# One decoder layer on one core: the gate stage in five rounds instead of four, with half of the output normed and stored in the last round

## The chip, the cores and the metric

The kernel runs on one core of a Trainium2 chip. The metric is the device time of one execution in microseconds (us). Five engines work side by side, each on its own list of instructions in order: PE (matrix products into the PSUM banks, with a separate track PEld for its weight loads), DVE (VectorE), ACT (ScalarE), POOL (GpSimd) and SP, which here only issues DMAs. They wait for each other by semaphores alone.

## The reference, cut to what matters

The last two steps of one decoder layer are the stage at issue; D = 2048, 512 tokens, depth 1.

```
h = h + y @ w_out                                     # mixer, before
h = h + square(relu(rmsnorm(h, g_mlp) @ w_up)) @ w_down   # MLP, before
gate = sigmoid(rmsnorm(h, g_ple) @ w_pg)              # w_pg: 2048 x 2048
h = h + gate * (p @ w_pp)                             # p: 512 x 256, w_pp: 256 x 2048
return rmsnorm(h, g_final)                            # mean of squares over 2048 columns
```

Everything is fp32. A product is made of three matmuls (`tri`): each operand is split into a part rounded to fp32r ("hi") and the rest ("lo"), and hi*hi, hi*lo and lo*hi are summed in a bank.

## The kernel before, in words

Tokens lie in four tiles of 128 (t = 0 to 3). In the gate stage h lies with tokens on the partitions, and is updated in 16 blocks: `block_of_h(q, t)` is 128 tokens by the 512 columns of quarter q.

The stage is a loop over the quarters q = 0 to 3. One quarter is nine half units (`GATE_HUS`, pos 0 to 8): eight for `w_pg` (each 256 of the 2048 rows by 512 columns) and, at pos 4, one for `w_pp`. A half unit has one weight half, which ACT copies to `w_hi` (`gate_hi`), DVE subtracts to `w_lo` (`gate_lo`), and PE multiplies with all four token tiles (`gate_half`): 4 tiles x 2 x 3 = 24 matmuls of 128x512, so 6 per tile. There are four slots of `w_hi` and `w_lo`, and `gate_hi` of a half unit waits until PE is done with the one four before:

```
act.wait_ge(half_done, s - 3)      # gate_hi
pe.wait_ge(half_lo, s + 1)         # gate_half
```

After pos 8 of quarter q its banks hold the gate's argument. It is worked off tile by tile while PE multiplies for quarter q + 1: `gate_clamp` (DVE, reads the bank), `gate_exp` (ACT), `gate_inverse` (ACT: a Ln and an Exp), `gate_add` (DVE: two steps of refinement, the product with pp, the sum into h), `square_out` (ACT: squares of the new block, summed into `x_sum`) and `gain_out` (DVE: the block times `g_final`). `gates_of(q, at)` says after which position of the next quarter each engine does which of these; it does them in three portions, at = 2, 3 and 4. The order of DVE and ACT is that of the program text, and nothing in it is skipped: an instruction that waits holds all those behind it.

The last quarter has no next one. Its gates stand behind the loop, then come the row means (`row_mean`), 1/sqrt (`rms_ln_exp` on ACT, `refine` on DVE), the scaling of each token tile of h by its row's factor (DVE t = 0, 1, 2; ACT t = 3), and the four stores of 1 MB each by SP.

```
for t in (0, 3, 1, 2):             # SP, behind the last load
    ... wait for the scaling of tile t
    sp.dma_start(out_tok[:, t, :]..., h[:, :, t * P:(t + 1) * P])
```

`w_pg` comes in 16 loads of 1 MB (a quad: two half units) into a ring of three (`load_quad`); a load is issued when `gate_lo` has read the second half of the quad three before.

## Time and profile before

| | us |
|---|---|
| median of 3 runs (lowest, highest) | 2589.91 (2589.11, 2590.95) |
| the profiled execution | 2590.34 |
| its span, first to last instruction | 2588.6 |
| PE busy in the span | 2506.7 (97%) |
| DVE busy | 1658.9 (64%) |
| ACT busy | 993.0 (38%) |
| POOL busy | 239.2 (9%) |

PE's granted clock is 0.987 of full speed on average. The page's first part gives busy time by engine; its second shows PE at 9 tenths or more in every slice but the first and the last; the last slice has 3 tenths. A time such as 2545.25 below is counted from the start of the span. In a row of the timeline the first number is the start, the second the length, "x3" says that three such instructions are merged, and what stands in brackets is how long the engine was idle before and what released it. In a row of "windows" come PE, PEld, DVE, ACT and POOL busy (with the number of instructions), then PE's granted clock (1.00 is 2.4 GHz, 0.50 is 1.2 GHz), the DMA engines' share and GB/s.

### The profile page before, as it was taken

The numbers are of one execution on the slowest core, as the hardware profiler recorded it, in microseconds if no ns is written. First come the engines' busy times: TensorE is split into PE (matmuls) and PEld (weight loads), VectorE is DVE, ScalarE is ACT, GpSimd is POOL, SyncE is SP. The second block draws the span as 40 slices with busy tenths as digits, with TensorE's granted clock in tenths as the row PEclk, the third lists the DMA queues.
The fourth block names the chain that finished last, engine by engine and source line by source line (L and its number), as shares of the span: only waits on it lengthen the run. The fifth ranks groups of instructions, "written<-read, shape, count | busy, mean of one in ns | idle before, by whom it ended". The sixth has DMA issues, their size and how long they took to land.

```text
span 2588.6 us, 29850 instructions
## 1 busy us (share of the span) xinstructions
PE 2506.7 (97%) x11424; PEld 2067.7 (80%) x11424; DVE 1658.9 (64%) x1995; ACT 993.0 (38%) x1338; POOL 239.2 (9%) x186
## 2 busy tenths in 40 slices
PE   6999999999999999999999999999999999999993
PEld 5788888888777788888888888888888888888883
DVE  5676666687778524444444444469898899894563
ACT  5444444334444213333333333334333333344442
POOL 5111111122023333000000000000000000000000
PEclk8999999999999999999999999999999999999997
DMA  6323223222232432655555555567555655633222
GB/s 213 82 65 81 74 72 81 74 73 76 70 81 74 138 97 81 203 183 176 176 182 182 183 183 182 180 226 258 197 174 195 244 216 207 225 133 111 85 74 65
DMA packets 414844, 366.93 MB, mean 142 GB/s; under 512 B 5356, under 2 KB 352136, under 8 KB 414616
## 3 DMA queue, kind: packets, MB, share of 16 engines
q1 hardware_dynamic: 414648, 365.54, 44.5%
q8 instruction: 67, 1.10, 0.2%
q14 instruction: 33, 0.27, 0.0%
q10 hardware_dynamic: 96, 0.02, 0.0%
HBM read 298.43 MB, written 67.11 MB: 141 GB/s over the span
## 4 chain that ended last, share of the span: by engine, by line
PE 64%; DVE 2%; ACT 1%; issue 0%; POOL 0%; DVEq 0%; POOLq 0%
PE bank L1757 21%; PE bank L1758 21%; PE bank L1759 21%; DVE u_lo L1501 0%; PE bank L1997 0%; PE bank L1953 0%; ACT w_hi L734 0%; DVE w_lo L1141 0%; DVE w_lo L1553 0%; ACT u_hi L901 0%; DVE gate_e L1679 0%; DVE gate_e L1675 0%; DVE gate_e L1673 0%; DVE h L1750 0%; DVE w_raw L1578 0%
## 5 line engine op out<-in xcount | busy, mean ns | idle before, releaser
L1757 PE MATMUL bank<-u_hi,w_hi 128*128 128x512 f32 x2192 | 874.5, 399 | 17.2 <-DVE w_lo L1141 6.3
L1759 PE MATMUL bank<-u_hi,w_lo 128*128 128x512 f32 x2192 | 858.4, 392 | 0.0
L1758 PE MATMUL bank<-u_lo,w_hi 128*128 128x512 f32 x2192 | 857.9, 391 | 0.0
L1757 PEld LDWEIGHTS bank<-u_hi,w_hi 128*128 128x128 f32 x2192 | 414.1, 189 | 112.2 <-issue 13.3
L1758 PEld LDWEIGHTS bank<-u_lo,w_hi 128*128 128x128 f32 x2192 | 414.4, 189 | 87.6 <-issue 4.6
L1759 PEld LDWEIGHTS bank<-u_hi,w_lo 128*128 128x128 f32 x2192 | 413.8, 189 | 87.4
L1141 DVE TENSOR_TENSOR w_lo<-w_raw,w_hi 128x2048 fp32r<-128x2048 f32 x132 | 307.5, 2329 | 209.2 <-ACT w_hi L734 209.1
L1757 PE MATMUL bank<-w_hi,forms 128*128 128x512 f32 x896 | 349.7, 390 | 0.4 <-DVE h L1596 0.4
L1759 PE MATMUL bank<-w_hi,forms 128*128 128x512 f32 x896 | 349.1, 390 | 0.0
L1758 PE MATMUL bank<-w_lo,forms 128*128 128x512 f32 x896 | 349.0, 389 | 0.0
L734 ACT ACTIVATE w_hi<-w_raw 128x2048 fp32r<-128x2048 f32 x137 | 260.5, 1904 | 226.2 <-PE bank L1759 212.2
L989 ACT ACTIVATE w_hi<-ring 128x1024 fp32r<-128x1024 f32 x128 | 136.4, 1066 | 213.6 <-PE bank L1759 146.1
L1757 PEld LDWEIGHTS bank<-w_hi,forms 128*128 128x128 f32 x896 | 168.3, 188 | 35.4 <-issue 0.8
L1759 PEld LDWEIGHTS bank<-w_hi,forms 128*128 128x128 f32 x896 | 168.3, 188 | 34.9
L1758 PEld LDWEIGHTS bank<-w_lo,forms 128*128 128x128 f32 x896 | 168.3, 188 | 34.6
L1516 DVE SCALAR_TENSOR_TENSOR relu<-bank,rs_u 128x512 f32<-128x512 f32 x64 | 44.3, 692 | 225.0 <-PE bank L1759 225.0
L962 ACT ACTIVATE araw<-relu 128x512 f32<-128x512 f32 x64 | 40.5, 633 | 351.2 <-DVE relu L1516 351.2
L1553 DVE TENSOR_TENSOR w_lo<-ring,w_hi 128x1024 fp32r<-128x1024 f32 x128 | 155.7, 1222 | 10.5 <-ACT w_hi L989 10.5
L989 ACT ACTIVATE w_hi<-w_raw 128x1024 fp32r<-128x1024 f32 x96 | 101.8, 1063 | 151.1 <-PE bank L1759 147.8
L689 POOL TENSOR_TENSOR tmp<-b 128x512 f32<-128x512 f32 x84 | 96.6, 1155 | 544.2 <-DVE ql L1251 244.1
L1596 DVE TENSOR_TENSOR h<-h,bank 128x512 f32<-128x512 f32 x224 | 143.3, 682 | 0.0
L1553 DVE TENSOR_TENSOR w_lo<-w_raw,w_hi 128x1024 fp32r<-128x1024 f32 x96 | 117.4, 1223 | 39.1 <-ACT w_hi L989 39.0
(234 smaller groups left out, 2508.8 us busy)
## 6 DMA issues: line engine op xcount, KB each, us to landing
w_raw<-in_w_up SPq DMA_DIRECT2D x64, 1024.0 KB, 6.4
w_raw<-in_w_in SPq DMA_DIRECT2D x57, 1024.0 KB, 5.6
forms_scratch<-stage SPq DMA_DIRECT2D x32, 1792.0 KB, 7.3
forms<-forms_scratch SPq DMA_DIRECT2D x56, 1024.0 KB, 7.2
ring<-in_w_down SPq DMA_DIRECT2D x40, 1024.0 KB, 5.9
w_raw<-in_w_down SPq DMA_DIRECT2D x24, 1024.0 KB, 5.5
w_raw<-in_w_out SPq DMA_DIRECT2D x16, 1024.0 KB, 5.9
ring<-in_w_pg SPq DMA_DIRECT2D x16, 1024.0 KB, 5.0
```

The lines of the kernel that those rows point to most:

```text
L689: pool.tensor_tensor(tmp[:, lv % 2, :].rearrange("q (n c) -> q n c", c=2 << lv), bv, ref, ALU.subtract).then_inc(diff_ready, 1)
L734: act.activation(w_hi[:, unit.slot, :], w_raw[:, unit.slot, :], ACT.Copy).then_inc(w_hi_ready, 1)
L962: act.activation(araw[:, i % 4, :], relu[:, i % 2, :], ACT.Square).then_inc(a_ready, 1)
L989: act.activation(hi_half(s), part(half_of(G, l), i), ACT.Copy).then_inc(half_hi, 1)
L1141: v.tensor_tensor(w_lo[:, unit.slot, :], w_raw[:, unit.slot, :], w_hi[:, unit.slot, :].bitcast(F32), ALU.subtract).then_inc(w_lo_ready, 1)
L1516: v.scalar_tensor_tensor(out=relu[:, i % 2, :], in0=bank[unit.slot][:, :], scalar=0.0, in1=rs_u[:], op0=ALU.max, op1=ALU.mult).then_inc(z_ ...
L1553: v.tensor_tensor(lo_half(s), part(half_of(G, l), l % 2), hi_half(s).bitcast(F32), ALU.subtract)\
L1596: v.tensor_tensor(dst, dst, by_tile(bank[bk + t][:, :]), op).then_inc(added, 1)
L1757: pe.matmul(ps, whi, xhi, start=start, stop=False, skip_group_check=shared)
L1758: pe.matmul(ps, whi, xlo, start=False, stop=False, skip_group_check=shared)
L1759: return pe.matmul(ps, wlo, xhi, start=False, stop=stop, skip_group_check=shared)
```

## The change

The quarter q = 3 is made in two rounds, first for token tiles 0 and 1, then for tiles 2 and 3. Both rounds go through all nine half units, so that each of these weight halves is loaded, copied and subtracted twice (pp's raw half is kept and only split again); a round of two tiles has 12 matmuls in a half unit. The gates of tiles 0 and 1 are worked off in the last round, which also norms, scales (tile 0 on DVE, tile 1 on ACT) and stores these two tiles; behind the last matmul the gates, the norm, the scaling and the stores of tiles 2 and 3 are left, with tile 3 scaled half by ACT and half by DVE and stored in two halves. The product with `g_final` moves to POOL for 14 of the 16 blocks. The portions of `gates_of` are spread over more positions, on both engines, and `gate_inverse` follows its own `gate_exp` directly.

```diff
+ROUNDS = ((0, (0, 1, 2, 3)), (1, (0, 1, 2, 3)), (2, (0, 1, 2, 3)), (3, (0, 1)), (3, (2, 3)))
+LAST = len(ROUNDS) - 1
...
+        def round_of(q, t):
+
+            return q + (q == NT - 1 and t >= 2)
...
-            return 5 * NT * q + (1, 2, 7, 12)[t]
+            return 5 * NT * q + ((1, 2, 7, 12) if q < NT - 1 else (1, 2, 11, 12))[t]
...
-            return 5 * NT * q + (6, 11, 16, 20)[t]
-
-        def gate_hu(q, pos):
-            return GATES + GATE_HUS * q + pos
+            return 5 * NT * q + ((6, 11, 16, 20) if q < NT - 1 else (6, 10, 16, 20))[t]
+
+        def round_done(q, t):
+
+            return sum(len(tiles) - 1 for _, tiles in ROUNDS[:round_of(q, t)]) + ROUNDS[round_of(q, t)][1].index(t) + 1
...
-            for n in range(3, 4 * NT):
-                q, i = n // 4, n % 4
+            for n in range(3, 4 * (LAST + 1)):
+                r, i = n // 4, n % 4
                 before, last = (n - 3) // 4, (1, 3, 6, 8)[(n - 3) % 4]
-                load_quad(q, i, gate_hu(before, last) + 1)
-                if i == 0:
-                    sp.wait_ge(half_lo, gate_hu(q - 1, 4) + 1)
-                    load_pp(q)
-
-            for t in (0, 3, 1, 2):
-                if t == NT - 1:
-                    sp.wait_ge(tok_scaled_act, 1)
-                else:
-                    sp.wait_ge(tok_scaled, t + 1)
-                sp.dma_start(out_tok[:, t, :].rearrange("q (m f) -> q m f", m=KT),
-                             h[:, :, t * P:(t + 1) * P]).then_inc(out_stored, 16)
-            sp.wait_ge(out_stored, 16 * NT)
+                load_quad(r, i, gate_hu(before, last) + 1)
+                if i == 0 and r < LAST:
+                    sp.wait_ge(half_lo, gate_hu(r - 1, 4) + 1)
+                    load_pp(r)
+
+            def store_out(t, k, n):
+                sp.dma_start(out_tok[:, t, k * P:(k + n) * P].rearrange("q (m f) -> q m f", m=n),
+                             h[:, k:k + n, t * P:(t + 1) * P]).then_inc(out_stored, 16)
+
+            sp.wait_ge(tok_scaled, 1)
+            store_out(0, 0, KT)
+            sp.wait_ge(tok_scaled_act, 1)
+            store_out(1, 0, KT)
+            sp.wait_ge(tok_scaled_act, 2)
+            store_out(3, 0, KT // 2)
+            sp.wait_ge(tok_scaled, 2)
+            store_out(2, 0, KT)
+            sp.wait_ge(tok_scaled, 3)
+            store_out(3, KT // 2, KT // 2)
+            sp.wait_ge(out_stored, 16 * (NT + 1))
...
+            pool.wait_ge(g_landed, 16)
+            for q in range(NT):
+                for t in range(NT):
+                    if q == NT - 1 and t >= 2:
+                        continue
+                    pool.wait_ge(out_squared, NT * q + t + 1)
+                    pool.tensor_tensor(block_of_h(q, t), block_of_h(q, t), by_tile(g_out[:, q * S:(q + 1) * S]), ALU.mult)\
+                        .then_inc(gained, 1)
...
+            def gates_of(r, at):
+
+                q, tiles = ROUNDS[r]
                 if at == 2:
-                    gate_exp(q, 0)
-                    gate_exp(q, 1)
-                    gate_inverse(q, 0)
+                    gate_exp(q, tiles[0])
+                    gate_inverse(q, tiles[0])
+                    gate_exp(q, tiles[1])
+                    gate_inverse(q, tiles[1])
+                if len(tiles) == 2:
+                    if at == 3:
+                        square_out(q, tiles[0])
+                    if at == 4:
+                        square_out(q, tiles[1])
+                    return
+                if at == 3:
                     gate_exp(q, 2)
-                    gate_inverse(q, 1)
-                if at == 3:
+                    square_out(q, 0)
+                    gate_inverse(q, 2)
+                if at == 4:
                     gate_exp(q, 3)
-                    gate_inverse(q, 2)
-                    square_out(q, 0)
+                    square_out(q, 1)
                     gate_inverse(q, 3)
-                    square_out(q, 1)
-                if at == 4:
+                if at == 6:
                     square_out(q, 2)
                     square_out(q, 3)
 
-            for q in range(NT):
+            for r, (q, tiles) in enumerate(ROUNDS):
                 for pos in range(GATE_HUS):
-                    gate_hi(q, pos)
-                    if q:
-                        gates_of(q - 1, pos)
-                    if q == 0:
+                    gate_hi(r, pos)
+                    if r:
+                        gates_of(r - 1, pos)
+                    if r == 0:
...
+                    if r == LAST and pos == 5:
+                        rms_ln_exp([tok[:, i, 0:2] for i in range(3)], tok_step, 3, tok_act, 0)
+                    if r == LAST and pos == 6:
+                        act.wait_ge(tok_step, 7)
+                        act.wait_ge(gained, 14)
+                        act.activation(h[:, :, P:2 * P], h[:, :, P:2 * P], ACT.Copy,
+                                       scale=tok[:, 1, 1:2]).then_inc(tok_scaled_act, 1)
+            gates_of(LAST, 2)
+            gates_of(LAST, 3)
+            gates_of(LAST, 4)
+
+            rms_ln_exp([tok[:, i, 2:4] for i in range(3)], tok_step, 10, tok_act, 2)
+            act.wait_ge(tok_step, 14)
             t = NT - 1
-            act.activation(h[:, :, t * P:(t + 1) * P], h[:, :, t * P:(t + 1) * P], ACT.Copy,
+            act.activation(h[:, 0:KT // 2, t * P:(t + 1) * P], h[:, 0:KT // 2, t * P:(t + 1) * P], ACT.Copy,
                            scale=tok[:, 1, t:t + 1]).then_inc(tok_scaled_act, 1)
...
+            def gates_of(r, at):
+                q, tiles = ROUNDS[r]
                 if at == 2:
-                    gate_clamp(q, 0)
-                    gate_clamp(q, 1)
-                    gate_add(q, 0)
+                    gate_clamp(q, tiles[0])
+                    gate_clamp(q, tiles[1])
+                    gate_add(q, tiles[0])
+                if len(tiles) == 2:
+                    if at == 3:
+                        gate_add(q, tiles[1])
+                    return
+                if at == 3:
                     gate_clamp(q, 2)
                     gate_add(q, 1)
-                if at == 3:
+                if at == 4:
                     gate_clamp(q, 3)
                     gate_add(q, 2)
-                    gain_out(q, 0)
+                if at == 5:
                     gate_add(q, 3)
-                    gain_out(q, 1)
-                if at == 4:
-                    gain_out(q, 2)
-                    gain_out(q, 3)
...
+                    if r == LAST and pos == 4:
+                        v.wait_ge(out_squared, 14)
+                        tok_bufs = [tok[:, i, 0:2] for i in range(3)]
+                        row_mean(tok_bufs, 0, 2, tok_step, 0)
+                    if r == LAST and pos == 5:
+                        refine(tok_bufs, tok[:, 1, 0:2], tok_step, 3, tok_act, 2)
+                        v.wait_ge(tok_step, 7)
+                    if r == LAST and pos == 6:
+                        v.wait_ge(gained, 14)
+                        rows = h[:, :, 0:P]
+                        v.tensor_scalar(rows, rows, tok[:, 1, 0:1], None, ALU.mult).then_inc(tok_scaled, 1)
+            gates_of(LAST, 2)
+            gates_of(LAST, 3)
+
+            v.wait_ge(out_squared, 16)
+            tok_bufs = [tok[:, i, 2:4] for i in range(3)]
+            row_mean(tok_bufs, 2, 2, tok_step, 7)
+            gain_out(NT - 1, 2)
+            gain_out(NT - 1, 3)
+            refine(tok_bufs, tok[:, 1, 2:4], tok_step, 10, tok_act, 4)
+            v.wait_ge(tok_step, 14)
+            v.wait_ge(last_gained, 2)
+            rows = h[:, :, 2 * P:3 * P]
+            v.tensor_scalar(rows, rows, tok[:, 1, 2:3], None, ALU.mult).then_inc(tok_scaled, 1)
+            rows = h[:, KT // 2:KT, 3 * P:S]
+            v.tensor_scalar(rows, rows, tok[:, 1, 3:4], None, ALU.mult).then_inc(tok_scaled, 1)
...
-                        pe.wait_ge(gate_step, gate_clamped(q - 1, NT - 1))
+                        pe.wait_ge(gate_step, gate_clamped(q - 1, tiles[-1]))
                     else:
                         pe.wait_ge(added, GATES)
-                for t in range(NT):
...
-                    if pos == GATE_HUS - 1 and t < NT - 1:
+                    if t == tiles[-1]:
+                        last.then_inc(half_done, 1)
+                    elif pos == GATE_HUS - 1:
                         last.then_inc(gate_done, 1)
-                    if t == NT - 1:
-                        last.then_inc(half_done, 1)
                     if t in between:
                         between[t]()
...
```

Three places show how the order moves. The first is DVE in the round that follows quarter 2, from the addition of tile 0's gate on: `w_lo<-ring` is the weight half of pos 3, `w_lo<-pp_raw` of pos 4, a row `gate_e<-bank,rs_neg` a clamp. Before, tiles 2 and 3:

```order
L1673 SCALAR_TENSOR_TENSOR gate_e<-gate_e,gate_inv 128x512
L1675 SCALAR_TENSOR_TENSOR gate_e<-gate_e,gate_inv 128x512
L1679 SCALAR_TENSOR_TENSOR gate_e<-gate_e,pp 128x512
L1682 TENSOR_TENSOR h<-h,gate_e 128x4x128
L1665 TENSOR_SCALAR gate_e<-bank,rs_neg 128x512
L1673 SCALAR_TENSOR_TENSOR gate_e<-gate_e,gate_inv 128x512
L1675 SCALAR_TENSOR_TENSOR gate_e<-gate_e,gate_inv 128x512
L1679 SCALAR_TENSOR_TENSOR gate_e<-gate_e,pp 128x512
L1682 TENSOR_TENSOR h<-h,gate_e 128x4x128
L1653 TENSOR_TENSOR w_lo<-ring,w_hi 128x1024
L1665 TENSOR_SCALAR gate_e<-bank,rs_neg 128x512
```

And now:

```order
L1715 SCALAR_TENSOR_TENSOR gate_e<-gate_e,gate_inv 128x512
L1717 SCALAR_TENSOR_TENSOR gate_e<-gate_e,gate_inv 128x512
L1721 SCALAR_TENSOR_TENSOR gate_e<-gate_e,pp 128x512
L1724 TENSOR_TENSOR h<-h,gate_e 128x4x128
L1695 TENSOR_TENSOR w_lo<-ring,w_hi 128x1024
L1707 TENSOR_SCALAR gate_e<-bank,rs_neg 128x512
L1715 SCALAR_TENSOR_TENSOR gate_e<-gate_e,gate_inv 128x512
L1717 SCALAR_TENSOR_TENSOR gate_e<-gate_e,gate_inv 128x512
L1721 SCALAR_TENSOR_TENSOR gate_e<-gate_e,pp 128x512
L1724 TENSOR_TENSOR h<-h,gate_e 128x4x128
L1695 TENSOR_TENSOR w_lo<-pp_raw,w_hi 128x1024
L1707 TENSOR_SCALAR gate_e<-bank,rs_neg 128x512
```

Tile 2's clamp and tile 1's addition now stand behind pos 3, tile 3's clamp behind pos 4; no `h<-h,g_out` is left on DVE here.

The second is DVE in the last round, from its pos 4 on (`tok` is the row factor, `h<-h,tok` the scaling of tile 0). Before, pos 4 to 8 were followed by the gates of the whole quarter:

```order
L1653 TENSOR_TENSOR w_lo<-pp_raw,w_hi 128x1024
L1687 TENSOR_TENSOR h<-h,g_out 128x4x128 x2
L1653 TENSOR_TENSOR w_lo<-ring,w_hi 128x1024 x4
L1665 TENSOR_SCALAR gate_e<-bank,rs_neg 128x512 x2
L1673 SCALAR_TENSOR_TENSOR gate_e<-gate_e,gate_inv 128x512
```

Now the norm and the scaling for tiles 0 and 1 stand between the positions:

```order
L1695 TENSOR_TENSOR w_lo<-pp_raw,w_hi 128x1024
L1756 TENSOR_TENSOR x_sum<-x_sum 128x2x2
L1756 TENSOR_TENSOR x_sum<-x_sum 128x2
L1192 TENSOR_SCALAR tok<-x_sum 128x2
L1695 TENSOR_TENSOR w_lo<-ring,w_hi 128x1024
L1197 TENSOR_TENSOR tok<-tok 128x2
L1199 TENSOR_TENSOR tok<-tok 128x2
L1201 TENSOR_SCALAR tok<-tok 128x2
L1203 TENSOR_TENSOR tok<-tok 128x2
L1695 TENSOR_TENSOR w_lo<-ring,w_hi 128x1024
L1798 TENSOR_SCALAR h<-h,tok 128x16x128
L1695 TENSOR_TENSOR w_lo<-ring,w_hi 128x1024 x2
```

The third is SP from the loads for quarter 1 on. Before:

```order
L547 DMA ring<-in_w_pg 128x4x512 x4
L550 DMA pp_raw<-in_w_pp 128x2x512
L547 DMA ring<-in_w_pg 128x4x512 x4
L550 DMA pp_raw<-in_w_pp 128x2x512
L547 DMA ring<-in_w_pg 128x4x512 x3
L601 DMA out<-h 2048x1x128 x4
```

Now there are four more loads (7 in place of 3 in the last row of them), and the stores are five:

```order
L558 DMA ring<-in_w_pg 128x4x512 x4
L561 DMA pp_raw<-in_w_pp 128x2x512
L558 DMA ring<-in_w_pg 128x4x512 x4
L561 DMA pp_raw<-in_w_pp 128x2x512
L558 DMA ring<-in_w_pg 128x4x512 x7
L608 DMA out<-h 2048x1x128 x2
L608 DMA out<-h 128x8x128
L608 DMA out<-h 2048x1x128
L608 DMA out<-h 128x8x128
```

All stores still stand behind the last load. POOL, which had nothing in this stage, ends with `TENSOR_TENSOR h<-h,g_out 128x4x128` fourteen times, each behind the squares of its block.

## Rows read from the trace of the kernel before

**Rows 1.** The page's part 4, shares of the chain that ended last.
```profile
PE 64%; DVE 2%; ACT 1%; issue 0%; POOL 0%; DVEq 0%; POOLq 0%
```
**Rows 2.** Windows over quarters 2 and 3 of the gate stage and over the end.
```profile
2447.00:2497.00 50.00, 50.00 (x219) 40.91 (x218) 27.02 (x35) 21.54 (x33) 0.00 (x0) 1.00 0.28 95
2497.00:2549.00 52.00, 52.00 (x228) 42.43 (x226) 24.05 (x32) 20.54 (x34) 0.00 (x0) 1.00 0.00 1
2549.00:2571.00 22.00, 0.29 (x2) 0.00 (x0) 16.33 (x30) 9.28 (x20) 0.00 (x0) 0.56 0.00 0
```
**Rows 3.** Timeline, PE: its last matmul.
```profile
2548.90 0.39 PE L1759 MATMUL bank<-w_hi,x 128*128 128x512 f32 x1
```
**Rows 4.** Timeline, DVE, the end.
```profile
2545.25 0.75 DVE L1665 TENSOR_SCALAR gate_e<-bank,rs_neg 128x512 f32<-128x512 f32 x1 [15.36 <-PE bank L1759]
2546.61 0.75 DVE L1665 TENSOR_SCALAR gate_e<-bank,rs_neg 128x512 f32<-128x512 f32 x1 [0.61 <-PE bank L1759]
2549.42 0.69 DVE L1673 SCALAR_TENSOR_TENSOR gate_e<-gate_e,gate_inv 128x512 f32<-128x512 f32 x1 [2.06 <-ACT gate_inv L1068]
2551.60 0.69 DVE L1682 TENSOR_TENSOR h<-h,gate_e 128x512 f32<-128x512 f32 x1
...
2568.59 0.36 DVE L1711 TENSOR_TENSOR x_sum<-x_sum 128x8 f32<-128x8 f32 x2
...
2570.46 3.68 DVE L1750 TENSOR_SCALAR h<-h,tok 128x2048 f32<-128x2048 f32 x3
```
**Rows 5.** Timeline, ACT, the end.
```profile
2546.03 0.63 ACT L1056 ACTIVATE gate_e<-gate_e 128x512 f32<-128x512 f32 x1 [15.46 <-DVE gate_e L1665]
...
2547.93 0.71 ACT L1065 ACTIVATE gate_inv<-gate_e,ln_scale_col 128x512 f32<-128x512 f32 x1
2548.67 0.72 ACT L1068 ACTIVATE gate_inv<-gate_inv,ln_shift_col 128x512 f32<-128x512 f32 x1
...
2566.90 0.63 ACT L1078 ACTIVATE squares<-h 128x512 f32<-128x512 f32 x1 [2.66 <-DVE h L1682]
2567.43 0.18 ACT L1078 ACTIVATION_READ_ACCUMULATOR squares<-h 128x1 f32 x1
```
**Rows 6.** Timeline, SP: the four stores.
```profile
2571.77 10.00 SPq L601 DMA_DIRECT2D out<-h  x4
```
**Rows 7.** The stores, line 601: from issue to landing.
```profile
DMA to landing us min/median/max: 5.5/9.3/10.4
```
**Rows 8.** A window within the stores.
```profile
2575.00:2580.00 5.00, 0.00 (x0) 0.00 (x0) 0.00 (x0) 0.00 (x0) 0.00 (x0) 0.50 0.98 282
```
**Rows 9.** Timeline, DVE: tiles 0 and 1 clamped after quarters 1 and 2.
```profile
2446.92 1.40 DVE L1665 TENSOR_SCALAR gate_e<-bank,rs_neg 128x512 f32<-128x512 f32 x2
...
2496.52 1.40 DVE L1665 TENSOR_SCALAR gate_e<-bank,rs_neg 128x512 f32<-128x512 f32 x2
```
**Rows 10.** Timeline, ACT: weight half of quarter 3, pos 2.
```profile
2494.28 1.06 ACT L1052 ACTIVATE w_hi<-ring 128x1024 fp32r<-128x1024 f32 x1 [4.38 <-PE bank L1759]
```
**Rows 11.** Groups by line and form, from 2340 us on: `gate_lo`.
```profile
L1653 DVE TENSOR_TENSOR w_lo<-ring,w_hi 128x1024 fp32r<-128x1024 f32 x31 | 37.2, 1223 | 49.0 <-ACT w_hi L1052 48.7
```
**Rows 12.** Timeline near 603 us, POOL.
```profile
603.53 2.70 POOL L689 TENSOR_TENSOR tmp<-b 128x512 f32<-128x512 f32 x2 [6.14 <-DVE b L1226]
```
**Rows 13.** Timeline near 603 us, DVE beside it.
```profile
603.92 1.42 DVE L1179 SCALAR_TENSOR_TENSOR y<-ez,y 128x512 f32<-128x512 f32 x1
```
**Rows 14.** Line 689, POOL: nanoseconds min/median/max, first and last start.
```profile
L689 POOL TENSOR_TENSOR tmp<-b x84: 1039/1093/3086, 67.8 to 825.5; 128x512 f32<-128x512 f32 x84
```
**Rows 15.** The loads of `w_pg`, line 547: from issue to landing.
```profile
DMA to landing us min/median/max: 4.9/5.0/7.7
```
**Rows 16.** Windows where PE had gaps.
```profile
660.00:664.00 4.00, 3.27 (x11) 2.27 (x12) 3.82 (x3) 1.95 (x2) 0.00 (x0) 0.61 0.07 12
664.00:668.00 4.00, 4.00 (x12) 3.06 (x11) 3.26 (x6) 0.65 (x4) 0.00 (x0) 0.54 1.13 302
748.00:752.00 4.00, 2.84 (x13) 2.08 (x12) 4.00 (x3) 1.23 (x1) 0.00 (x0) 1.00 0.24 58
```

More of the change, by code:

```diff
@@ L542, in _, with load_quad @@
                 load_form(0, j)
-            def load_quad(q, i, after):
-                n = NT * q + i
+            def load_quad(r, i, after):
+                n, q = NT * r + i, ROUNDS[r][0]
                 sp.wait_ge(half_lo, after)
@@ L1039, in _, with gate_hi @@
                             turn_hi(l - 9)
-            def gate_hi(q, pos):
-                s = gate_hu(q, pos)
+            def gate_hi(r, pos):
+                s, q = gate_hu(r, pos), ROUNDS[r][0]
                 act.wait_ge(half_done, s - 3)
@@ L1643, in _, with gate_lo @@
                         turn_lo(l - 9)
-            def gate_lo(q, pos):
-                s = gate_hu(q, pos)
+            def gate_lo(r, pos):
+                s = gate_hu(r, pos)
                 v.wait_ge(half_hi, s + 1)
@@ L1716, in _, with row_sum @@
-            for q in range(NT):
+            def row_sum(first, n, step, at):
+                sums_of = x_sum[:, :].rearrange("q (a t) -> q a t", t=NT)[:, :, first:first + n]
+                for i, width in enumerate((2, 1)):
+                    if i:
+                        v.wait_ge(step, at + i)
+                    v.tensor_tensor(sums_of[:, 0:width, :], sums_of[:, 0:width, :], sums_of[:, width:2 * width, :], ALU.add)\
+                        .then_inc(step, 1)
+                v.wait_ge(step, at + 2)
@@ L1717, in _, with row_mean @@
+            def row_mean(buf, first, n, step, at):
+                row_sum(first, n, step, at)
+                mean_square(buf, x_sum[:, first:first + n], D, step)
+            for r, (q, tiles) in enumerate(ROUNDS):
                 for pos in range(GATE_HUS):
-                    s = gate_hu(q, pos)
+                    s = gate_hu(r, pos)
                     if s in (GATES + 1, GATES + 3):
                         add_products((s - 5) // 2)
-                    gate_lo(q, pos)
-                    if q:
-                        gates_of(q - 1, pos)
@@ L1724, in _ @@
-                    if q == 0:
+                    gate_lo(r, pos)
+                    if r:
+                        gates_of(r - 1, pos)
+                    if r == 0:
                         if pos < 3:
@@ L2013, in _, with gate_half @@
                         turn(l - 5)
-            def gate_half(q, pos, between=()):
-                s = gate_hu(q, pos)
+            def gate_half(r, pos, between=()):
+                s, (q, tiles) = gate_hu(r, pos), ROUNDS[r]
                 whi, wlo = hi_half(s), lo_half(s)
@@ L2020, in gate_half @@
                 z = pos if pos < 4 else pos - 1
[L2021 removed]
+                if r == 0:
                     pe.wait_ge(xg_lo, KT + 2 if pos == 4 else 2 * z + 2)
@@ L2029, in gate_half @@
                     if q:
-                        pe.wait_ge(gate_step, gate_clamped(q - 1, NT - 1))
+                        pe.wait_ge(gate_step, gate_clamped(q - 1, tiles[-1]))
                     else:
                         pe.wait_ge(added, GATES)
-                for t in range(NT):
+                for t in tiles:
                     bk = bank[4 * (q % 2 if pos == 4 else (q + 1) % 2) + t][:, :]
@@ L2050, in turns @@
                 return {t: (lambda n=first + t: turn(n)) for t in range(NT)}
-            for q in range(NT):
+            for r in range(LAST + 1):
                 for pos in range(GATE_HUS):
                     between = ()
-                    if q == 0 and pos == 1:
+                    if r == 0 and pos == 1:
                         pe.wait_ge(added, GATES - 2)
                         between = turns(8)
-                    elif q == 0 and pos == 2:
+                    elif r == 0 and pos == 2:
                         pe.wait_ge(added, GATES)
                         between = turns(12)
-                    elif q == 0 and pos == 3:
+                    elif r == 0 and pos == 3:
                         pe.wait_ge(p_landed, 16)
                         between = {0: lambda: turn_p(0), 1: lambda: turn_p(1)}
-                    gate_half(q, pos, between)
+                    gate_half(r, pos, between)
 _INS = ["x", "p", "g_mix", "w_in", "lb_logits", "g_hg_norm", "conv_w", "w_gla_gate", "b_gla_gate", "g_gla_norm",
```

49 lines of the change are left out of this document (14 added, 35 removed).

## The prediction

> **What bounds the kernel now.** I read the chain that ended last first: 64% of it is PE and 2% and 1% are DVE and ACT [rows 1], so over almost all of the span only PE's work counts. The windows then part the gate stage from its end: PE is busy in all 52 us up to 2549, at clock 1.00, with DVE busy 24 and ACT 21 of them, and in the 22 us that follow PE does nothing, DVE works 16 and ACT 9 [rows 2]. PE's last matmul starts at 2548.90 and ends at 2549.3 [rows 3]. From there to the end, 2588.6, are 39.3 us in two parts. Up to the first store at 2571.77 DVE and ACT hand four tiles' gates to and fro, then norm them; after it 16.8 us are four stores of 1 MB each [rows 6]. The last quarter's tail is bare, since nothing is left for PE. The profiled execution took 2590.34, which is 1.74 more than its span and 0.43 more than the median, 2589.91. I make the sum on the span.
>
> **What the tail costs now and then.** Let E be 2549.3, the end of PE's work. In the new order tiles 2 and 3 alone are left. A tile's share of a half unit is 1.36 us, since the clamps released by PE are 1.36 apart (2545.25, 2546.61) [rows 4], so tile 2 is clamped at E - 1.33 = 2547.97. From a clamp to its Exp are 0.78 us, from the Ln to the second Exp 0.74, from there to the addition 0.75 [rows 4, 5]; the Exp itself takes 0.63, and the Ln now follows it directly. So tile 2's addition starts at 2547.97 + 0.78 + 0.65 + 0.74 + 0.75 = 2550.89. An addition is four instructions, the last one 2.18 after the first, and frees DVE 0.6 later (independent instructions overlap by 0.1: two clamps of 0.75 take 1.40 [rows 9]): 2.79 in all. Tile 3's inverse is ready at about 2552.9, before DVE is free. So its addition starts at 2553.68 and ends 2.87 later at 2556.55; the squares take 0.71 with their read [rows 5]: 2557.28. Before, from the first row sum to the first scaling were 1.87 us, of which DVE waited 0.5 for ACT [rows 4]; now two products with g_final stand in this gap at 0.6 each, which adds some 0.75: scaling starts at 2559.9. ACT scales half a tile, like a weight half of 1024 columns 1.06 us [rows 10], so the first store goes out at about 2561.0. Before it was 2571.77. That is **10.8 us** less.
>
> The stores: in the middle of them 282 GB/s are moved [rows 8]. 4.19 MB at that rate are 14.9 us, and 1.9 of the 16.8 are start and completion (a first store of 1.05 MB alone, 3.7 us at that rate, lands after 5.5 [rows 7], 1.8 more). Left behind the last matmul are 2.1 MB, 7.4 us less: **7.4 us**. SP issues the three within 1 us, so the queue has work throughout, and the stores of tiles 0 and 1, scaled behind `gate_lo` of the last round's pos 6 when PE has some three half units of 2.76 before it, go out some 8 us before E and have landed 9.4 later, well ahead of the first of these three. Both parts together make 18.2.
>
> **What PE loses for it.** The count of matmuls stays: a quarter takes 2496.52 - 2446.92 = 49.60 [rows 9], so two rounds of half the tiles take 24.8 each, 2.76 for a half unit. But DVE and ACT prepare each weight half in full. DVE needs 1.22 (one after the other 1.14) [rows 11], ACT 1.06: nine of them are 10.3 and 9 us out of 24.8 and fit. What doesn't fit is the round behind quarter 2, where four tiles' gates lie beside half the matmuls. DVE's sum there is 10.3 + 4 x (0.66 + 2.79) = 24.1, as much as the round; and it is no row of independent work. Positions 3, 4 and 5 are strung together: a tile's clamp, 0.78 to its Exp, 0.54, a square of 0.62, Ln 0.74, Exp 0.63, then the weight half on ACT, 1.09, then `gate_lo`, 1.14, behind which the next clamp stands: 5.5 us for a position, where PE takes 2.76. Before, PE took 5.5 too, which hid it.
>
> PE's lead covers part. ACT's weight half at 2494.28 was released by the end of quarter 2's pos 7 [rows 10], so quarter 2 ends at 2494.1 + 5.5 = 2499.6. Tiles 0 and 1 are clamped at 2496.52 [rows 9]; tile 0's addition starts at 2499.44, tile 1's inverse is done at 2501.4, then come ACT's and DVE's halves for pos 3, done at 2503.6; tile 2's clamp is at 2503.56, tile 3's 5.54 later at 2509.1, `gate_lo` of pos 5 starts 4.4 after that and ends at 2514.7. PE has done pos 0 to 4 at 2499.6 + 13.8 = 2513.4. It waits, a weight load of 0.2 included, 1.5 us. Then pos 6's half: tile 3's addition stands before it, 1.14 + 2.79 + 1.22 = 5.15 behind the start of pos 5's at 2513.5, hence 2518.7; PE is ready at 2514.9 + 2.76 = 2517.7 and waits 1.2. Behind this the halves come every 1.1 to 1.3 and PE's lead is back by the round's end. In the last round two gates alone are left, and by the same steps PE has 0.3 us to spare at its tightest place, pos 4. Loss so far: **2.7**.
>
> **POOL** takes over the products with g_final, 14 in all. In rounds 1 and 2 DVE has 23 us of slack in 50 [rows 2]. In the last two rounds there are six. The trace has no such product on POOL. The nearest rows are line 689, a subtraction of the same size: 1.04 at least, 1.09 in the median [rows 14], 2.70 for two that DVE works beside [rows 12]. It isn't free for DVE: beside those two a DVE instruction of 0.69 took 1.42 [rows 4, 13]. That is 0.73 lost for one on POOL, more than the 0.6 that the same product took on DVE.
> The Trainium skill has a rule for it ("SBUF — State Buffer", section "SBUF: two separate sides"): VectorE and GpSimd share one pair of ports, held for a whole instruction, and a VectorE instruction with two inputs in SBUF is locked out while GpSimd reads SBUF. The trace agrees with its 1.42 for 0.69. By the rule each product on POOL blocks the next addition or `gate_lo` for its whole length; with no lock the loss stays 2.7.
> On the path this matters at two places: the product of quarter 2, tile 2 falls into tile 3's addition ahead of pos 6, and that of quarter 3, tile 0 into tile 1's addition ahead of pos 4 in the last round. At 1.04 each that is 1.0 + (1.04 - 0.3), with 0.1 of the others: 1.9. At 1.35 each, half of the 2.70, and with more of them touching the path, it is 3.4; the low end is 0, if none meets. I take 2.3, near 1.09 to 1.2 for one, and so **5.0** for PE's loss, with 2.7 and 6.1 as ends.
>
> Other edits at nothing: the later clamp of tile 3 in rounds 1 and 2 (it frees PE's bank for pos 4, 22 us into a round; the clamp comes at 12); row means and scaling of tiles 0 and 1, 0.5 and 1.3 on DVE and 2.0 on ACT, which fall behind pos 4 to 6 of the last round, when the lead is three half units; the four more loads, which land in 5.0 [rows 15] and are asked for at least two half units, 5.5 us, ahead of use. If they took the 7.7 of the slowest, 1 to 2 us would be added. SP's stores stand behind all loads and hold none up.
>
> **Sum.** 2588.6 - 10.8 - 7.4 + 5.0 = 2575.4 for the span, 2577.1 with the 1.74; against the median 0.43 less. I say **2577**, 0.5% faster.
>
> **Rivals.**
> *A, no loss.* If DVE's and ACT's hand-over were quicker or POOL's products fell into idle time, PE would lose 0 to 2.7: 2572 to 2574.7. For it: DVE idles 2 us at each clamp to addition [rows 4]. Against: I followed the steps, and before shows each of them at these lengths. 0.12.
> *B, a short fall of the clock or late loads.* PE gets two gaps of 1.5 and 2.2 us within 7 us. With 3.27 and 4.00 us busy of 4 the granted clock was 0.61 and 0.54, that is mostly the 1.2 GHz level, and elsewhere with 2.84 of 4 it stayed at 1.00 [rows 16]. Such 8 us cost about 3.5; slow loads 2. 2580 to 2584: 0.14.
> *C, slower.* The clock falls at the first gap, near 2513, and stays at 1.2 GHz to the end of PE's work. 36 us of matmuls would then take 72, less the 5.0 of waiting that vanish: 2590.3 - 18.2 + 36 = 2608. It outweighs the 18.2 from some 36 us at half clock on. Against it: at half speed PE waits for nobody, is busy throughout, and the mean clock of 0.987 over the span before says that such stretches ended. 0.03.
> *D, the change doesn't do what it says.* The stores of tiles 0 and 1 leave late, since scaling waits for POOL's fourteenth product, and all 4.19 MB queue at the end: 7.4 of the gain gone, 2584.5. They would have to be over 10 us late; 0.04. With others of no effect, 0.02 more.
>
> **How the numbers follow.** My forecast, 2574.7 to 2580, has 0.65. The range of 8 in 10 leaves out C, D and part of B: 2572 to 2583. This kernel's measurement can tell 0.2%, 5.2 us, from no change. Faster than 2584.7 are the forecast, A, B and most of D: 0.93; same 0.03; slower 0.04.
>
> **What would show it.** In the changed trace PE should wait for `w_lo` twice in the first half round, before pos 5 and pos 6, 1.5 and 2.2 us, and at most once in the last; its last matmul should start near 2554. DVE instructions beside POOL's products should read 1.4 or more for 0.69. Two stores should be issued before PE ends and three about 11.7 after, and the span should end 21 after PE. I am wrong in the tail if that last distance is not 20 to 22.5, and in PE's loss if its waits sum to under 2 or over 8; a clock under 1.00 between 2500 and 2550 would be B or C.

## The result, and the profile after

| | before | after |
|---|---|---|
| median (lowest, highest), us | 2590.54 (2589.11, 2592.48), 6 runs | 2576.78 (2576.02, 2582.55), 6 runs |
| ratio, 95% interval | | 0.9949 [0.9939, 0.9959] |
| profiled execution | 2590.34 | 2582.55 |
| its span | 2588.6 | 2580.8 |
| PE, DVE, ACT, POOL busy | 2506.7, 1658.9, 993.0, 239.2 | 2513.7, 1671.2, 1004.1, 262.1 |

The change saves 0.5%, and 2577 had been forecast. The profiled execution of the changed kernel is the slowest of its six, so its span must not be set against the old one as a whole. The clamps of quarter 2 show where the excess lies. They started at 2496.52 before [rows 9] and start at 2500.89 now. From DVE's timeline of the changed kernel (start, length, then line, operation and tiles; in brackets the idle time before it and its releaser), the first row is that clamp of quarter 2, the others are the last tile's clamp, the row sums and the last scaling:

```profile
2500.89 1.40 DVE L1707 TENSOR_SCALAR gate_e<-bank,rs_neg 128x512 f32<-128x512 f32 x2
...
2558.61 0.75 DVE L1707 TENSOR_SCALAR gate_e<-bank,rs_neg 128x512 f32<-128x512 f32 x1 [3.97 <-PE bank L1822]
2559.97 0.75 DVE L1707 TENSOR_SCALAR gate_e<-bank,rs_neg 128x512 f32<-128x512 f32 x1 [0.61 <-PE bank L1822]
...
2568.00 0.36 DVE L1756 TENSOR_TENSOR x_sum<-x_sum 128x4 f32<-128x4 f32 x2 [0.79 <-ACT squares L1105]
...
2570.46 1.29 DVE L1811 TENSOR_SCALAR h<-h,tok 128x2048 f32<-128x2048 f32 x1
```

Here 4.4 us were lost before the parts that the change could hurt, and over the profiles of all kernels below this clamp starts anywhere from 2493.55 to 2500.89, with an unchanged program for the first 2380 us and always 99.20 us from quarter 0's clamps to quarter 2's. So the 4.4 arise earlier. In this execution PE's clock fell for a stretch near 876 us in which it had stood in the profile before. Windows of core 0, with the columns of [rows 2], the changed kernel:

```profile
876.00:880.00 4.00, 3.34 (x8) 2.61 (x9) 3.81 (x3) 0.00 (x0) 3.81 (x2) 0.62 0.51 143
```

The same 4 us of the kernel before:

```profile
876.00:880.00 4.00, 4.00 (x20) 3.30 (x19) 1.06 (x1) 0.00 (x0) 3.26 (x2) 1.00 1.11 305
```

The granted clock is 0.62 in the one and 1.00 in the other. POOL's timeline has the same two instructions on either side of this stretch, which tell its price. Before:

```profile
875.11 2.86 POOL L719 TENSOR_TENSOR sq_tmp<-h 128x512 f32 x1 [0.19 <-POOL sum_sq L721]
886.17 1.04 POOL L719 TENSOR_TENSOR sq_tmp<-h 128x512 f32 x1 [6.84 <-DVE h L1482]
```

After:

```profile
877.85 2.86 POOL L737 TENSOR_TENSOR sq_tmp<-h 128x512 f32 x1 [0.19 <-POOL sum_sq L739]
890.55 1.04 POOL L737 TENSOR_TENSOR sq_tmp<-h 128x512 f32 x1 [8.47 <-DVE h L1524]
```

The changed kernel is 2.7 us late at the first and 4.4 at the second, and 4.4 it stays up to quarter 2's clamps. So this place cost 1.6. Read from the same timelines, 1.1 of the rest is there by 812 us, and 1.7 comes between 834 and 868 us, where the granted clock of 856 to 860 is 0.52 after and 1.00 before.

So I measure within a profile, from landmark to landmark. From the clamps of quarter 2 to the clamp of the last tile (here 2559.97) PE does the same work in every kernel. Before it is 2496.52 to 2545.25 + 3 x 1.36 = 2549.33 [rows 4, 9], 52.81 us; after it is 59.08. **PE lost 6.3 us.** From the last clamp to the end the old tail is 39.3, the new one 2580.8 - 2559.97 = 20.8. **The tail gave 18.4 us.** The difference, 12.2, less the 4.4 lost upstream is the 7.8 between the spans.

The timeline of PE shows its loss (start, length; the brackets give the wait):

```profile
2517.58 0.39 PE L1822 MATMUL bank<-w_hi,p_lo 128*128 128x512 f32 x1
2519.21 0.50 PE L1820 MATMUL bank<-w_hi,x 128*128 128x512 f32 x1 [1.24 <-DVE w_lo L1695]
...
2521.88 0.39 PE L1822 MATMUL bank<-w_hi,x 128*128 128x512 f32 x1
2524.09 0.50 PE L1820 MATMUL bank<-w_hi,x 128*128 128x512 f32 x1 [1.83 <-DVE w_lo L1695]
...
2525.59 0.63 PE L1820 MATMUL bank<-w_hi,x 128*128 128x512 f32 x1
2526.02 0.63 PE L1821 MATMUL bank<-w_lo,x 128*128 128x512 f32 x1
```

Starts are normally 0.23 apart. Before pos 5 of the first half round the distance is 1.63, before pos 6 it is 2.21, and in the last round, before pos 4, 0.99: gaps of 1.40, 1.98 and 0.76, and 0.1 more at the matmul behind each, 4.5 in all. From 2525.59 on eight matmuls start 0.43 apart, which is the 1.2 GHz level, and cost 1.6 us more. Together that is 6.1 of the 6.3.

DVE's timeline in the same place:

```profile
2510.07 0.69 DVE L1721 SCALAR_TENSOR_TENSOR gate_e<-gate_e,pp 128x512 f32<-128x512 f32 x1
2510.80 1.67 DVE L1724 TENSOR_TENSOR h<-h,gate_e 128x512 f32<-128x512 f32 x1
```

and POOL's beside it:

```profile
2510.07 1.84 POOL L747 TENSOR_TENSOR h<-h,g_out 128x512 f32<-128x512 f32 x1 [34.06 <-ACT squares L1105]
```

The addition of 0.69 takes 1.67 while POOL's product runs, and the product 1.84. All 14 on POOL took 1.29 to 1.85. Each of the six in the two half rounds stretches what DVE does beside it: four times a step of an addition, to 1.66, 1.67 or 1.78, once a `w_lo` of 1.22 to 1.62, and once the two row sums of 0.35 to 1.45.

POOL waits too. Its row above starts together with DVE's instruction before the addition and ends at 2511.91, 1.15 after that instruction's end (2510.07 + 0.69). The same holds for all six: each ends 1.14 to 1.16 after the end of the DVE instruction with two inputs in SBUF that ran when it started. So the product itself takes about 1.15, and what its row has beyond that is waiting for DVE.

The tail's own steps are in ACT's timeline. Behind the rows of `tok` ACT scales half a tile:

```profile
2570.46 1.15 ACT L1175 ACTIVATE h<-h,tok 128x1024 f32<-128x1024 f32 x1 [1.42 <-DVE tok L1203]
```

The first of the last three stores follows its end (the queue's timeline has them as one row from 2571.63), and the span ends 9.2 us later.

### The profile page after: what moved, and what is told of

It is laid out like the page before. It is cut to its first block, busy times and chain, and to the rows that moved or that the text cites. A ratio compares the mean times of both kernels' runs of the same rounds, so it can differ in the third digit from the quotient of the medians.

```text
span 2580.8 us, 29882 instructions
## 1 busy us (share of the span) xinstructions
PE 2513.7 (97%) x11424; PEld 2070.8 (80%) x11424; DVE 1671.2 (65%) x1997; ACT 1004.1 (39%) x1350; POOL 262.1 (10%) x200
## 4 chain that ended last, share of the span: by engine, by line
PE 63%; DVE 3%; ACT 1%; issue 0%; POOL 0%; DVEq 0%; POOLq 0%; ACTq 0%
PE bank L1820 21%; PE bank L1821 21%; PE bank L1822 21%; DVE u_lo L1543 0%; PE bank L2016 0%; PE bank L2060 0%; DVE h L1724 0%; DVE w_lo L1695 0%; ACT w_hi L761 0%; DVE gate_e L1717 0%; DVE gate_e L1715 0%; DVE w_lo L1183 0%; ACT w_hi L1079 0%; DVE gate_e L1721 0%; DVE gate_e L1707 0%
## 5 line engine op out<-in xcount | busy, mean ns | idle before, releaser
L1820 PEld LDWEIGHTS bank<-u_hi,w_hi 128*128 128x128 f32 x2192 | 414.6, 189 | 113.4 <-issue 13.8
L747 POOL TENSOR_TENSOR h<-h,g_out 128x512 f32<-128x512 f32 x14 | 22.9, 1640 | 1485.3 <-ACT squares L1105 1485.3
L1595 DVE TENSOR_TENSOR w_lo<-ring,w_hi 128x1024 fp32r<-128x1024 f32 x128 | 155.6, 1221 | 10.5 <-ACT w_hi L1016 10.5
```

The costliest lines, as they stand in the source:

```text
L747: pool.tensor_tensor(block_of_h(q, t), block_of_h(q, t), by_tile(g_out[:, q * S:(q + 1) * S]), ALU.mult)\
L1595: v.tensor_tensor(lo_half(s), part(half_of(G, l), l % 2), hi_half(s).bitcast(F32), ALU.subtract)\
L1820: pe.matmul(ps, whi, xhi, start=start, stop=False, skip_group_check=shared)
```

## The experiments

In all of them I read the same landmarks. The diffs are cut to what matters. "Loss" is the time from quarter 2's clamps to the last tile's, less 52.81. The gaps are distances between PE's starts, less 0.23.

| kernel | time, us | ratio to before, interval | loss | PE's gaps | clock |
|---|---|---|---|---|---|
| after, first profile | 2576.78 | 0.9949 [0.9939, 0.9959] | 6.3 | 1.40, 1.98, 0.76 | 8 slow |
| e_after_again | 2578.78 | 0.9952 [0.9939, 0.9966] | 6.2 | 1.40, 2.03, 0.75 | 8 slow |
| e_no_product | 2575.16 | 0.9938 [0.9922, 0.9955] | 3.0 | 1.35, 1.03, 0.15 | full |
| e_later | 2577.14 | 0.9941 [0.9925, 0.9958] | 4.8 | 2.12 (pos 7), 0.76 | 8 slow |
| e_later_no_product | 2573.40 | 0.9931 [0.9914, 0.9947] | 0.0 | none | full |
| e_dve_product | 2574.80 | 0.9938 [0.9919, 0.9956] | 3.9 | 1.34, 1.01, 1.07 | full |
| e_stores_end | 2584.45 | 0.9976 [0.9966, 0.9987] | 5.4 | 1.40, 2.03, 1.56 | full |
| e_before_order | 2585.17 | 0.9978 [0.9969, 0.9987] | 0 | none | full |
| e_fused | 2573.90 | 0.9933 [0.9920, 0.9947] | 1.1 | 0.23, 0.52 | full |
| e_fused_halves | 2571.52 | 0.9922 [0.9909, 0.9936] | 0.0 | none | full |

("8 slow": that many matmuls 0.43 apart behind the gaps.) The rows down to e_dve_product differ in time by less than their intervals are wide; what tells them apart is the profile, and there is one of each. The kernels from e_stores_end to e_fused share their chip and their runs of the kernel before with e_after_again; e_no_product, e_later, e_later_no_product and e_dve_product share theirs.

**e_no_product.** PE's loss has two supposed causes. This takes POOL's away. Left out: the factor g_final in 14 of the 16 blocks.

```diff
-                    pool.tensor_tensor(block_of_h(q, t), ..., by_tile(g_out[:, q * S:(q + 1) * S]), ALU.mult)
-                        act.wait_ge(gained, 14)
-                        v.wait_ge(gained, 14)
```


> The changed kernel without the 14 products with g_final on POOL (14 of the 16 blocks of the output lack that factor). Theory: PE's waits in the two half rounds have two causes, the chain clamp to w_lo through DVE and ACT (positions 5 and 6 of the first half round) and POOL's products, which hold DVE's additions up. Without POOL the waits fall from about 4.5 to 2.7 us (1.5 before pos 5, 1.2 before pos 6, none in the last round), every addition on DVE reads 0.69, and the time is 1.5 to 2 us under the changed kernel's. Rival: POOL costs DVE nothing that PE notices; the waits stay at 4 to 4.5.

The gap before pos 5 stays (1.35), the one before pos 6 halves, the one in the last round all but goes. The additions read 0.69 again. DVE's timeline of e_no_product at position 4 to 5:

```profile
2507.66 1.23 DVE L1686 TENSOR_TENSOR w_lo<-pp_raw,w_hi 128x1024 fp32r<-128x1024 f32 x1 [0.85 <-ACT w_hi L1071]
2508.80 0.75 DVE L1698 TENSOR_SCALAR gate_e<-bank,rs_neg 128x512 f32<-128x512 f32 x1
2509.46 0.68 DVE L1706 SCALAR_TENSOR_TENSOR gate_e<-gate_e,gate_inv 128x512 f32<-128x512 f32 x1
...
2511.63 0.69 DVE L1715 TENSOR_TENSOR h<-h,gate_e 128x512 f32<-128x512 f32 x1
2513.18 1.23 DVE L1686 TENSOR_TENSOR w_lo<-ring,w_hi 128x1024 fp32r<-128x1024 f32 x1 [0.86 <-ACT w_hi L1071]
```

These rows are the chain itself. From one `w_lo` to the next are 5.52 us, where PE takes 2.76 for a position. DVE works in 4.7 of them and is idle for 0.86, waiting for ACT's weight half. So both the bunching of an addition and a clamp in one position and the hand-over through ACT make it long; whether DVE's sum over the whole round would bound too is left to e_later_no_product. The waits are 2.6 in the first half round, where 2.7 were expected, and 0.25 in the last, where none was. The rival that POOL costs nothing fell.

**e_later.** The other cause alone: the gates of quarter 2 further apart, so that no position has to wait for the whole string. POOL as it is.

```diff
 ACT gates_of, quarter 2                 DVE gates_of, quarter 2
-  at 3: exp 2, square 0, inverse 2     -  at 4: clamp 3, add 2
-  at 4: exp 3, square 1, inverse 3     -  at 5: add 3
-  at 6: square 2, square 3
+  at 4: exp 2, inverse 2               +  at 4: clamp 3
+  at 5: exp 3, inverse 3, square 0     +  at 5: add 2
+  at 7: square 1, square 2             +  at 6: add 3
+  at 8: square 3
```


> The changed kernel with the gates of quarter 2, tiles 2 and 3, one position further apart on both engines (ACT: pos 4 and 5 in place of 3 and 4, squares at 5, 7 and 8; DVE: additions at 3, 5 and 6), POOL's products as they are. Theory: the chain no longer runs through a position, so the waits of 1.5 and 2.1 us before pos 5 and 6 go; POOL's products then meet DVE before pos 7 and cost 2 to 3 us there and about 1 before pos 4 of the last round: 3 to 4.5 in all, little better than the changed kernel. Rival: DVE's total work bounds the round, whatever its order: 4.5 or more, at pos 5 and 6 as before.

Pos 5 and 6 have no gap any more. POOL's products are now met before pos 7 (2.12), and the one of the last round stays. These waits are 3.0 together, at the low end of the expected 3 to 4.5. With a clock that fell right behind the one long gap the loss is 4.8 for 6.2, little better, as expected.

**e_later_no_product.** Both.

> Both edits: the gates of quarter 2 spread further and no products with g_final on POOL (14 of the 16 blocks lack that factor). Theory: both causes are gone, PE waits nowhere in the two half rounds (under 0.3 us), and the time is about 4.5 us under the changed kernel's, 2572. Rival, DVE's total work: it is 24 us in a round of 24.8, so that 1 to 3 us of waits stay.

No gap: 2495.91 to 2548.71 (DVE's timeline, below) are 52.80, to the hundredth the length of the full rounds before. The two causes together explain all of PE's waits, and splitting each weight half twice costs nothing by itself. The expected 2572 was 2573.4, within its spread of 2571.75 to 2574.68. The rival, DVE's sum over the round as the bound, fell: the sum is the same as in e_no_product, and only its distribution differs.

```profile
2495.91 1.40 DVE L1712 TENSOR_SCALAR gate_e<-bank,rs_neg 128x512 f32<-128x512 f32 x2
...
2548.71 0.75 DVE L1712 TENSOR_SCALAR gate_e<-bank,rs_neg 128x512 f32<-128x512 f32 x1 [0.61 <-PE bank L1838]
```

**e_dve_product.** The products back on DVE, at positions 6 and 7 (for the two tiles, 3 and 4).

```diff
+                if at == 6:
+                    gain_out(q, 0)
+                    gain_out(q, 1)
+                if at == 7:
+                    gain_out(q, 2)
+                    gain_out(q, 3)
```


> The changed kernel with the 14 products back on DVE (for a full quarter at positions 6 and 7, for the two tiles of the last round at 3 and 4), nothing on POOL. Theory: the chain's 1.5 and 1.2 stay, and 1.2 us of products before pos 7 and again before pos 8 eat the rest of the lead: 3 to 3.8 us of waits, less than with POOL. Rival: POOL takes work off DVE as meant, and DVE alone does worse than the changed kernel, over 4.5 us of waits.

The loss is 3.9, and the clock stood. With POOL it is 5.4 where the clock stood as well (e_stores_end, below). So moving the products to POOL didn't relieve DVE; in the profiles it cost 1.5 more than it saved. The times, with overlapping intervals, don't tell the two apart. The gaps were not quite where I had put them: pos 7 and 8 have none, and the last round's pos 4 waits 1.07.

**e_after_again.** The changed kernel once more, beside the next three.

> The changed kernel unchanged, as the reference of this group. 2576 to 2578 us. Theory: PE's waits in the half rounds are again 4.4 to 4.6 us in the profile; whether the clock falls behind them (3.4 us of matmuls at 0.43 in place of 0.23 in the first profile, 1.6 us lost) differs between executions. Rival: the fall always follows the two gaps, in this profile too.

Gaps and clock repeat, also the loss, 2498.30 to 2557.32; the median is 0.8 above the expected range. This profile alone would leave the rival standing, that the fall always follows the gaps. But e_stores_end has the same first two gaps, to the hundredth, and no slow matmul behind them. The fall is not bound to the gaps alone. Its net price is under 1.6: in e_stores_end PE then waits 1.56 before pos 4 of the last round, in e_after_again, where it comes later to that point, 0.75. Losses of 6.2 and 5.4 make 0.8.

**e_stores_end.** The stores' part of the tail.

```diff
             sp.wait_ge(tok_scaled, 1)
-            store_out(0, 0, KT)
-            sp.wait_ge(tok_scaled_act, 1)
-            store_out(1, 0, KT)
             sp.wait_ge(tok_scaled_act, 2)
             store_out(3, 0, KT // 2)
+            store_out(0, 0, KT)
+            store_out(1, 0, KT)
```


> The changed kernel with the stores of tiles 0 and 1 held back until tile 3's first half is scaled: all 4.19 MB go out behind the last matmul. Theory: the bytes count at 282 GB/s, so it is 7.4 us slower than the changed kernel, near 2584.2, and from the first store to the end are 16.5 to 17 us in place of 9.2. Rival: with five stores queued the engines move more per us, or the end is latency, and it costs under 4 us.

The last tile is clamped at 2554.55 and the span ends at 2582.8: 28.2 for 20.8, **7.4 us**, as in the sum. The window of e_stores_end in the midst of them (the last two columns are the DMA engines' share and GB/s) reads:

```profile
2568.00:2578.00 10.00, 0.00 (x0) 0.00 (x0) 0.00 (x0) 0.00 (x0) 0.00 (x0) 0.50 0.97 283
```

The DMA engines are full at 283 GB/s, so two more stores of 1 MB cost their transfer, 2.10 MB / 283 GB/s = 7.4. The medians of e_stores_end and e_after_again are 5.7 apart, less than this: here the clock stood behind the gaps (0.8), and the rest is within the spread between executions.

**e_before_order.** The other part of the tail. How much of it needs the split, and how much only another order?

```diff
-            gates_of(NT - 1, 2)
-            gates_of(NT - 1, 3)
-            gates_of(NT - 1, 4)
+            gate_clamp(q, 0)
+            gate_clamp(q, 1)
+            gate_add(q, 0)
+            gate_clamp(q, 2)
+            gate_clamp(q, 3)
+            for t in range(1, NT):
+                gate_add(q, t)
+                gain_out(q, t - 1)
+            gain_out(q, NT - 1)
```
(and on ACT each `gate_inverse` directly behind its `gate_exp`)

> The kernel before, with another order in its tail alone: behind the last matmul each Ln follows its own Exp on ACT, and DVE clamps tiles 2 and 3 together and adds tile after tile; four full rounds, four stores at the end. Theory: by the same steps as in the prediction the first row sum comes at 2563.3 in place of 2568.6 of the profile before, 5.3 us earlier, without a loss on PE: near 2585.2. So half of the 10.8 us between last matmul and first store would be had by order alone. Rival: the handing to and fro is not what bounds the tail, the number of tiles is: under 2 us gained.

DVE's timeline of e_before_order, from the first tile's clamp over the other clamps to the row sums:

```profile
2546.23 0.75 DVE L1673 TENSOR_SCALAR gate_e<-bank,rs_neg 128x512 f32<-128x512 f32 x1 [15.36 <-PE bank L1774]
...
2549.92 0.69 DVE L1683 SCALAR_TENSOR_TENSOR gate_e<-gate_e,gate_inv 128x512 f32<-128x512 f32 x1
...
2551.98 1.41 DVE L1673 TENSOR_SCALAR gate_e<-bank,rs_neg 128x512 f32<-128x512 f32 x2
...
2564.39 0.35 DVE L1719 TENSOR_TENSOR x_sum<-x_sum 128x8 f32<-128x8 f32 x2
```

DVE works almost without a pause: it waits 0.85 before the first addition and 0.26 before the last product. In the kernel before it waited 2.06 before each of the first three additions, the first shown in [rows 4]. DVE's timeline of before has the other two:

```profile
2555.02 0.69 DVE L1673 SCALAR_TENSOR_TENSOR gate_e<-gate_e,gate_inv 128x512 f32<-128x512 f32 x1 [2.06 <-ACT gate_inv L1068]
...
2560.61 0.69 DVE L1673 SCALAR_TENSOR_TENSOR gate_e<-gate_e,gate_inv 128x512 f32<-128x512 f32 x1 [2.06 <-ACT gate_inv L1068]
```

There ACT made a tile's Ln and second Exp only behind the Exp of the next tile. For tile 0 that meant waiting for tile 1's clamp, which PE releases 1.36 later; for tiles 1 and 2 the next clamp stood on DVE behind the addition before, so that the two engines waited for each other in turn. From clamp to row sums were 2568.59 - 2545.25 = 23.34 [rows 4]; now it is 18.16, 5.2 less, where 5.3 were expected. The median is 6.5 under that of before on the same chip, and its interval, 0.9969 to 0.9987, has room for 5.2.

**e_fused.** Meant as a version that beats both: the order of e_later, and the factor g_final inside the scaling. DVE scales all four tiles, tiles 2 and 3 in halves, and ACT none.

```diff
-                v.tensor_scalar(rows, rows, tok[:, 1, 0:1], None, ALU.mult)      # and 14 products on POOL
+                v.scalar_tensor_tensor(out=rows, in0=rows, scalar=tok[:, 1, t:t + 1],
+                                       in1=by_tile(g_out[:, k * P:(k + n) * P]), op0=ALU.mult, op1=ALU.mult)
```


> Meant as a faster version: five rounds, the gates of quarter 2 spread as in e_later, and the product with g_final nowhere by itself: the scaling does both in one DVE instruction of three operands (rows times factor times g_final), for tiles 0 and 1 in the last round and for tiles 2 and 3 in four halves at the end, with six stores. POOL and ACT do nothing for it. Theory: no waits of PE (under 0.5 us; the scaling of one tile is 2.2 us on DVE, which has about 4 us to spare in the last round), two products less in the tail (0.75 us), so 5 us faster than the changed kernel, near 2571.7. Rival: the 2.2 us pieces on DVE make PE wait in the last round instead, 1 to 3 us, and half the gain is lost.

It is 4.9 under e_after_again, but not free: one tile's scaling holds DVE for 2.35, and PE waits 0.23 and 0.52 in the last round, 1.1 with what is slow behind them. The rival had that. The time missed 2571.7 by 2.2. DVE's timeline of e_fused in the last round:

```profile
2538.35 2.35 DVE L1722 SCALAR_TENSOR_TENSOR h<-h,tok,g_out 128x2048 f32<-128x2048 f32 x1
2541.76 2.34 DVE L1722 SCALAR_TENSOR_TENSOR h<-h,tok,g_out 128x2048 f32<-128x2048 f32 x1
```

**e_fused_halves.** The same work in halves behind positions 5 to 8.

```diff
-                    if r == LAST and 5 <= pos < 7:
-                        scale_out(pos - 5, 0, KT)
+                    if r == LAST and 5 <= pos < 9:
+                        scale_out((pos - 5) // 2, (pos - 5) % 2 * (KT // 2), KT // 2)
```


> e_fused with the scaling of tiles 0 and 1 in halves of 1024 columns behind positions 5, 6, 7 and 8 of the last round, in place of whole tiles of 2.35 us behind 5 and 6. In e_fused PE waited 0.9 us there (before pos 6 and 7). Theory: DVE has the time in sum, only the piece was too long; the waits go to under 0.2 us and the time is 1 us under e_fused's, near 2573. Rival: DVE's sum in the last round is the bound, and the waits only move to pos 7 and 8, 0.7 us or more.

No gap is left, 2498.05 to 2550.85 are 52.80, and 2571.52 is the fastest of all: 0.9922 [0.9909, 0.9936] of before, 5.3 us under the changed kernel's median, or 7 by the two ratios. Its interval ends just below those of the changed kernel (0.9936 against 0.9939). DVE's timeline of e_fused_halves shows the halves apart, with room for a `w_lo` between them:

```profile
2539.19 1.28 DVE L1722 SCALAR_TENSOR_TENSOR h<-h,tok,g_out 128x1024 f32<-128x1024 f32 x1
2541.53 1.28 DVE L1722 SCALAR_TENSOR_TENSOR h<-h,tok,g_out 128x1024 f32<-128x1024 f32 x1
```

## Why the prediction was right, point by point

*The tail up to the first store.* Forecast: scaling 10.6 after the end of PE's work, the first of the last stores 11.7 after it. It came 10.5 and 11.6 after the last clamp. The steps from clamp to addition held too: 0.78, 0.65, 0.74, 0.75 were said, and tile 2 has 0.79, 0.66, 0.76, 0.75. What the prediction didn't part is the reason for these 10.8 us. e_before_order shows 5.2 for the order of Exp, Ln and clamps, which needed no fifth round. The other half is what is left of the 10.8, by subtraction: tiles that are out of the way.

*The stores.* Forecast 7.4; e_stores_end gives 7.4.

*PE's waits.* Forecast 1.5 and 2.2 before pos 5 and 6 of the first half round, and 0.8 before pos 4 of the last, with POOL's part at 1.04 each; found 1.5, 2.1 and 0.9 with what follows each gap. Without POOL it was to be 2.7; e_no_product gives 2.6, and 0.25 in the last round, where 0.3 to spare had been said. That the third wait fits is luck. It was measured behind the fallen clock; with the clock up, in e_stores_end, PE waits 1.56 there, twice what was said. Of it 1.4 comes with POOL's products (0.15 without them), where one product of 1.04 was counted. At full clock the loss is 5.4, near the 5.0 of the sum, and POOL's part of it 5.4 - 3.0 = 2.4, where 2.3 was taken.

*POOL.* The rule cited from the Trainium skill ("SBUF — State Buffer", section "SBUF: two separate sides"), by which each product would block DVE's next instruction with two inputs in SBUF, holds: 1.67 for 0.69, and both causes had to go before the loss did. One product was taken at 1.04 to 1.2 from a neighbour. Its rows read 1.29 to 1.85, which seems a miss, but those of the half rounds hold POOL's own waits for DVE. From DVE's release on it is 1.14 to 1.16 there, as taken, and a DVE instruction that starts with it loses about 1 us.

*The clock.* Part of rival B happened: the clock fell behind a gap of about 2 us in three of the four profiles that have one (in e_later behind that single gap), for 8 matmuls, at a net price of 0.8 and not 3.5. With it the loss in the profile was 6.3, where 5.0 was said, 6.1 being the upper end. So the profiles give 12.2 for the gain, the forecast was 13.2, and the medians are 13.8 apart. That the median came out at 2577 to 0.2 us is luck, within a spread between executions that is larger than these errors. Slow loads, the other half of B, did not occur: the slowest of the 20 landed after 7.6 us, and no weight half of ACT in the two half rounds waited for one.

*The slower rival C* asked for a clock that stays down. It returned after eight matmuls, with PE busy throughout, as argued. *D:* the stores of tiles 0 and 1 were issued from 2551.74, 8.2 us before the last clamp.

## What to carry to other kernels

When work of a fixed size per block (splitting, copying) stays and the matmuls beside it are halved, add up not only each engine's busy time, but the string from one block's hand-over to the next one's; here the sum fitted (24.1 of 24.8) and the string did not (5.5 for 2.76), and spreading its links over more blocks removed the wait at no cost, once POOL's products were gone as well. Moving an elementwise product from DVE to GpSimd was no relief here, where DVE is the tight one and has two-input work at the same time; folding it into an instruction that passes over the same data anyway was. And before a tail is cut by more rounds, look whether its order alone keeps two engines waiting in turn: that was worth 5.2 of 10.8 us.
